# Gathering the rows of experts 4 to 7 in two halves of two experts, on one Trainium2 core

## The reference, cut to what matters

```python
expert = g_top * EXPERTS_PER_GROUP + top_i          # two experts for each token
xb = x_pad[idx]                                     # the rows of one expert
hb = jax.nn.silu(xb @ w_gate[e]) * (xb @ w_up[e])   # 1024 -> 512, twice
return hb @ w_down[e]                               # 512 -> 1024
y = jnp.zeros((n + 1, d), x.dtype).at[tok_pad].add(contrib)
```

## Time and profile before

| what | value |
|---|---|
| median of 3 runs | 1997.57 us (1997.38 to 1999.03) |
| the profiled execution's own time | 2002.36 us |
| its span in the profile | 2000.6 us |
| TensorE busy | 1926.9 us (96%) |
| VectorE busy | 803.8 us (40%) |
| ScalarE busy | 432.4 us (22%) |
| weight loads of experts (2 MB each) | 192 |

### The profile page before, as it was taken

The page is one execution under the profiler, slowest core; times in us unless marked ns, Lnnn a source line. Parts: engine busy times, 40 slices in busy tenths (PEclk is TensorE's granted clock), DMA queues, the critical chain, the costliest instruction groups (busy, mean ns, idle before and its releaser), DMA issues.

```text
span 2000.6 us, 21987 instructions
## 1 busy us (share of the span) xinstructions
PE 1926.9 (96%) x8606; PEld 1004.3 (50%) x8606; DVE 803.8 (40%) x2057; ACT 432.4 (22%) x883; POOL 87.5 (4%) x116
## 2 busy tenths in 40 slices
PE   8999999999999889999999999999988999999998
PEld 6886644444444335544454444444433564654555
DVE  4553454221111144455544422211114548874564
ACT  2000101111111024165310111111112532124454
POOL 0000000000000010023000000000001000000000
PEclk9999899999999899999999999999989999999999
DMA  7815489999999981121548999999999221120000
GB/s 309 195 69 231 167 338 405 428 427 427 428 428 427 425 345 67 73 85 42 230 169 346 408 428 427 428 428 429 427 424 358 79 90 67 60 85 1 12 11 22
DMA packets 48550, 512.32 MB, mean 256 GB/s; under 512 B 5296, under 2 KB 7472, under 8 KB 19248
## 3 DMA queue, kind: packets, MB, share of 16 engines
q1 hardware_dynamic: 39984, 480.86, 59.0%
q0 software_dynamic: 8448, 29.89, 3.9%
HBM read 484.38 MB, written 26.35 MB: 255 GB/s over the span
## 4 chain that ended last, share of the span: by engine, by line
PE 86%; DMA 5%; DVE 4%; ACT 2%; issue 2%; POOL 1%; SPq 0%; DVEq 0%; POOLq 0%; ACTq 0%
PE ps L1099 22%; PE ps L1138 10%; PE ps L1072 8%; PE ps L522 6%; PE ps L1949 6%; PE ps L728 5%; PE ps L1499 5%; PE ps L1666 3%; PE ps L2284 3%; PE ps L2147 3%; PE ps L1697 2%; DMA ring<-in_wexp 2%; PE ps L1163 1%; PE ps L2321 1%; PE ps L2302 1%
## 5 line engine op out<-in xcount | busy, mean ns | idle before, releaser
L1099 PE MATMUL ps<-ring,arena 128*48 128x512 f32 x1504 | 390.6, 607 | 29.4 <-issue 17.5
L1099 PEld LDWEIGHTS ps<-ring,arena 128*48 128x48 f32 x1504 | 116.3, 125 | 224.5 <-issue 223.1
L1112 DVE TENSOR_TENSOR arena<-arena,ps 48x512 f32<-48x512 f32 x64 | 44.2, 690 | 451.4 <-ACT arena L1106 451.3
L1072 PEld LDWEIGHTS ps<-arena,h 128*128 128x128 f32 x1024 | 158.6, 190 | 44.6 <-issue 44.6
L1138 PE MATMUL ps<-ring,arena 128*48 128x512 f32 x768 | 173.6, 592 | 1.1 <-ACT arena L1126 0.6
L1072 PE MATMUL ps<-arena,h 128*128 128x192 f32 (+1 forms) x1024 | 174.3, 325 | 0.0
L1099 PE MATMUL ps<-arena 128*48 128x512 f32 x544 | 173.0, 608 | 0.9 <-issue 0.9
L1106 ACT ACTIVATE arena<-ps 48x512 f32<-48x512 f32 x64 | 37.8, 590 | 465.4 <-PE ps L1099 465.4
L1949 PE MATMUL ps<-ring,arena 128*128 128x512 f32 (+3 forms) x384 | 132.7, 500 | 0.8 <-DVE arena L360 0.8
L1499 PE MATMUL ps<-ring,arena 128*128 128x512 f32 x256 | 114.0, 601 | 6.5 <-issue 3.3
L728 PE MATMUL ps<-ring,arena 128*128 128x512 f32 x256 | 112.8, 594 | 0.1
(11 more groups left out here) (301 smaller groups left out, 2307.7 us busy)
## 6 DMA issues: line engine op xcount, KB each, us to landing
ring<-in_wexp SPq DMA_DIRECT2D x142, 2048.0 KB, 19.5
arena<-in_wexp SPq DMA_DIRECT2D x50, 2048.0 KB, 16.1
ring<-in_wall SPq DMA_DIRECT2D x25, 2048.0 KB, 8.7
y_d<-arena POOLq DMA_DIRECT2D x60, 192.0 KB, 7.1
yo_d<-gbuf SPq DMA_DIRECT2D x2, 4032.0 KB, 46.4
ring<-in_wall SPq DMA_DIRECT2D x3, 1536.0 KB, 7.4
xs_d<-h POOLq DMA_DIRECT2D x8, 512.0 KB, 7.3
ring<-in_wall SPq DMA_DIRECT2D x4, 1024.0 KB, 7.4
```

The source lines that it names most:

```text
L1072: mm = pe.matmul(banks[4 + t % 2][:, k * 4 * CAP + z0:(k + 1) * 4 * CAP], h[:, i, kk * P:(kk + 1) * P], RT["sel"][:, NT * (p_ % 2) + i, z0 ...
L1099: mm = pe.matmul(outs[m], xeT[:, e_ // 4 % 2, k, e_ % 4 * CAP:(e_ % 4 + 1) * CAP], ws[m][:, k, :], start=(k == 0), stop=(k == KT - 1))
L1112: dve.tensor_tensor(hh[0:CAP, e_ % 2, :], sl[0:CAP, e_ % 2, :], banks[1][64:64 + CAP, :], ALU.mult).then_inc(S["hh"], 1)
```

## The change

The steps of a gather now carry the range of experts of the quad that they take, (p_, q_, za, zb). Quad 1 is gathered in eight steps of two experts (96 columns) instead of four steps of four (192 columns). The four steps of experts 4 and 5 stand at e = 2 and e = 3, where the whole quad's stood. The four of experts 6 and 7 stand at e = 4 (two) and e = 5 (two), ahead of quad 2's first and second step. `rows_done` gives the count of copies that an expert waits for, and quad 3's selection matrix is made at e = 6 instead of e = 4, since its buffer is read by quad 1 until e = 5.

```diff
+        XT_AT = [[], [(0, q_, 2, 4) for q_ in range(4)], [(1, 0, 0, 2), (1, 1, 0, 2)], [(1, 2, 0, 2), (1, 3, 0, 2)]]
+        XT_AT += [[(e_ // 4 + 1, e_ % 4, 0, 4)] if e_ // 4 + 1 < NE // 4 else [] for e_ in range(4, NE)]
+        XT_AT[4][0:0] = [(1, 0, 2, 4), (1, 1, 2, 4)]
+        XT_AT[5][0:0] = [(1, 2, 2, 4), (1, 3, 2, 4)]
+        XT_NO = {step: t for t, step in enumerate(step for steps_ in XT_AT for step in steps_)}
+
+        def rows_done(e_):
+
+            if e_ < 2:
+                return 2
+            return 3 + max(t for (p_, q_, z0, z1), t in XT_NO.items() if p_ == e_ // 4 and z0 <= e_ % 4 < z1)
+
+
+        SEL_AT = {1: 2, 6: 3}
+        SEL_AT.update({4 * p_ - 8: p_ for p_ in range(4, NE // 4)})
...
-        def pe_xt(pe, l, p_, q_):
-            t = 4 * p_ + q_
-            z0 = 2 * CAP if p_ == 0 else 0
+        def pe_xt(pe, l, p_, q_, za, zb):
+            t = XT_NO[p_, q_, za, zb]
+            z0, z1 = za * CAP, zb * CAP
...
-                    mm = pe.matmul(banks[4 + t % 2][:, k * 4 * CAP + z0:(k + 1) * 4 * CAP], h[:, i, kk * P:(kk + 1) * P], RT["sel"][:, NT * (p_ % 2) + i, z0:],
+                    mm = pe.matmul(banks[4 + t % 2][:, k * 4 * CAP + z0:k * 4 * CAP + z1], h[:, i, kk * P:(kk + 1) * P], RT["sel"][:, NT * (p_ % 2) + i, z0:z1],
...
-            pe.wait_ge(*M("xtc", l, 1 if e_ < 2 else 4 * (e_ // 4) + 6))
+            pe.wait_ge(*M("xtc", l, 1 if e_ < 2 else rows_done(e_)))
...
-                if e_ == 1 or e_ >= 4 and e_ % 4 == 0 and e_ // 4 + 2 < NE // 4:
-                    dve_sel(dve, l, e_ // 4 + 2)
+                if e_ in SEL_AT:
+                    dve_sel(dve, l, SEL_AT[e_])
```

More of the change, by code:

```diff
@@ L113, in build @@
         yo_d = [dram(f"yo_d{l}", [CAP * NOVF, D]) for l in range(2)]
-        LAYER = dict(gu=NE, sl=NE, hh=NE, ht=NE, hTc=NE, dn=NE, ya=NE, yb=NE, xt=NE + 2, xtc=NE + 2, sel=NE // 4 + NT, pp=8, ppc=8, cmb=8, pg=8, pl_t=8, sg=8,
+        LAYER = dict(gu=NE, sl=NE, hh=NE, ht=NE, hTc=NE, dn=NE, ya=NE, yb=NE, xt=NE + 6, xtc=NE + 6, sel=NE // 4 + NT, pp=8, ppc=8, cmb=8, pg=8, pl_t=8, sg=8,
                      ple_h=8, r_mm=4, r_lg=4, r_oh=4, r_cum=3, r_cnt=5, r_dif=2, r_exp=2, hot=8, ixmm=1, ix=1, ovf=1, tw=1, tt=1, ttc=1, tmm=8, tadd=8,
@@ L1040, in build @@
         PT_AT = 11
-        XT_AT = [[], [(0, 0), (0, 1), (0, 2), (0, 3)], [(1, 0), (1, 1)], [(1, 2), (1, 3)]]
-        XT_AT += [[(e_ // 4 + 1, e_ % 4)] if e_ // 4 + 1 < NE // 4 else [] for e_ in range(4, NE)]
+        XT_AT = [[], [(0, q_, 2, 4) for q_ in range(4)], [(1, 0, 0, 2), (1, 1, 0, 2)], [(1, 2, 0, 2), (1, 3, 0, 2)]]
[9 more added lines that the diff above has]
+        SEL_AT.update({4 * p_ - 8: p_ for p_ in range(4, NE // 4)})
         def hT_of(j):
@@ L1055, in dve_sel @@
             if p_ >= 2:
-                dve.wait_ge(*M("xt", l, 4 * (p_ - 2) + 6))
+                dve.wait_ge(*M("xt", l, rows_done(4 * (p_ - 2) + 3)))
             for i in range(NT):
@@ L1071, in pe_xt, with dve_xt @@
                 for i in range(NT):
-                    mm = pe.matmul(banks[4 + t % 2][:, k * 4 * CAP + z0:(k + 1) * 4 * CAP], h[:, i, kk * P:(kk + 1) * P], RT["sel"][:, NT * (p_ % 2) + i, z0:],
+                    mm = pe.matmul(banks[4 + t % 2][:, k * 4 * CAP + z0:k * 4 * CAP + z1], h[:, i, kk * P:(kk + 1) * P], RT["sel"][:, NT * (p_ % 2) + i, z0:z1],
                                    start=(i == 0), stop=(i == NT - 1))
             mm.then_inc(S["xt"], 1)
-        def dve_xt(dve, l, p_, q_):
-            t = 4 * p_ + q_
-            z0 = 2 * CAP if p_ == 0 else 0
+        def dve_xt(dve, l, p_, q_, za, zb):
+            t = XT_NO[p_, q_, za, zb]
+            z0, z1 = za * CAP, zb * CAP
             g = gain_cols(1 + 3 * l)[:, 2 * q_:2 * q_ + 2]
@@ L1082, in dve_xt @@
                 dve.wait_ge(*M("gu", l, 4 * (p_ - 2) + 4))
-            dve.tensor_tensor(xeT[:, p_ % 2, 2 * q_:2 * q_ + 2, z0:], banks[4 + t % 2][:, 0:8 * CAP].rearrange("p (k c) -> p k c", k=2)[:, :, z0:],
-                              g.unsqueeze(2).broadcast_to([P, 2, 4 * CAP - z0]), ALU.mult).then_inc(S["xtc"], 1)
+            dve.tensor_tensor(xeT[:, p_ % 2, 2 * q_:2 * q_ + 2, z0:z1], banks[4 + t % 2][:, 0:8 * CAP].rearrange("p (k c) -> p k c", k=2)[:, :, z0:z1],
+                              g.unsqueeze(2).broadcast_to([P, 2, z1 - z0]), ALU.mult).then_inc(S["xtc"], 1)
         def pe_gu(pe, l, e_):
@@ L1173, in dve_turn @@
             st = steps(dve)
-            dve.wait_ge(*M("xt", l, NE + 2))
+            dve.wait_ge(*M("xt", l, NE + 6))
             st.did(dve.memset(selw, 0.0))
@@ L1220, in pe_moe @@
                     pe_down(pe, l, e_ - 1)
-                for p_, q in XT_AT[e_]:
-                    pe_xt(pe, l, p_, q)
+                for step in XT_AT[e_]:
+                    pe_xt(pe, l, *step)
                 if e_ == 7:
@@ L1264, in dve_moe @@
                     dve_down(dve, l, e_ - 1)
-                for p_, q in XT_AT[e_]:
-                    dve_xt(dve, l, p_, q)
-                if e_ == 1 or e_ >= 4 and e_ % 4 == 0 and e_ // 4 + 2 < NE // 4:
-                    dve_sel(dve, l, e_ // 4 + 2)
+                for step in XT_AT[e_]:
+                    dve_xt(dve, l, *step)
+                if e_ in SEL_AT:
+                    dve_sel(dve, l, SEL_AT[e_])
                 next(places, None)
@@ L1338, in ovf_begin @@
                 e.wait_ge(*M("xs", l, 16 * NT))
-                e.wait_ge(*M("xtc", l, NE + 2))
+                e.wait_ge(*M("xtc", l, NE + 6))
                 e.wait_ge(*M("hTc", l, OVF_AT + 1))
```

## The result

The changed kernel is slower by a little: 2002.66 us median of 20 runs (1997.82 to 2010.6) against 1997.21 us for the kernel before (20 runs, 1994.34 to 2000.77), ratio 1.0028, 95% interval 1.0020 to 1.0037. A second set of runs on another occasion, 11 of them, gave 1.0014 (1.0005 to 1.0023). So the two sets put the cost of the change at 0.14% and 0.28%, 2.8 and 5.6 us, and their intervals reach from 1.0 to 7.4 us; forecast were 2.9.

A forecast was written before the change was run, and what follows sets the result against it. The weight stream was taken to bound each layer, with time changing only at its pauses. Shifts of +1.3 us in layer 0 and +1.6 in layer 1 gave 1997.57 + 2.9 = 2000.5 us, range 1997.8 to 2003.8.

The forecast's parts named there:

- a smaller margin: At expert 9, less margin than taken: 1 us a layer more, +4.9 us in all; chance 0.12.
- What bounds the layer: Each layer ends when its weight stream ends; time is won or lost only where the stream pauses.
- The rest of TensorE's lag: Late in a layer, lag above the stream's shift (3.6 - 1.3) goes in TensorE's own waits for weights, about 2.3 us.
- TensorE's terms: Two 96-column steps take 3.66 us; TensorE stands -3.7 us from expert 4, 0.0 from expert 5, +3.6 from expert 6.
- The old pauses: Stream pauses at 300 and 315 us, worth 1.0 and 1.5 us, both go as TensorE is earlier.
- The first and second new pause: At experts 5 and 6, TensorE's shift less the margin puts the stream at -1.6, then +0.5 us.
- The third new pause: At expert 9, near 390 us in layer 0: stream shift of +1.3 us there and +1.6 us in layer 1.
- the 15.4 us: Landing time of a weight load on an empty queue, from loads of 15.3 and 15.5 us; anything above is margin.
- the margin at expert 9: How much later its load may be issued without a pause: 2.3 us in layer 0, 2.0 in layer 1.
- Rival A: Layer end hangs on TensorE, so its lag passes whole: 3.64 us a layer, 2004.9 us; chance 0.12.
- Rival C: No third pause at expert 9; the two before it cancel what was won: +0.5 a layer, 1998.6 us; chance 0.2.
- rival B: In the gather steps, a half-width matmul costs half (169 ns): -2.5 us a layer, 1992.6 us; chance 0.06.

The follow-up runs named there:

- e3: The changed kernel with all eight steps of quad 1's gather at e = 2 and e = 3, four at each; ratio 1.0035 to the kernel before.
- e6: The changed kernel with quad 3's gathers put later, to e = 10 and 11, and 128 instructions more in each layer's jumped-over block; ratio 1.0000 to the kernel before.
- e1: The changed kernel with 128 TensorE instructions more in each layer's first overflow block, which is jumped over; ratio 1.0013 to the kernel before.
- e7: The changed kernel unaltered, run again on another occasion; ratio 1.0014 to the kernel before.

## Why the prediction was right, and which term was too small

It held in its mechanism and in its direction, and was low by the last term: forecast were +2.9 us, the two layers measured +4.2, and the two sets of runs 2.8 and 5.6. What came is nearest to the case that the forecast gave 0.12, a smaller margin and +4.9 us.

- **What bounds the layer**: right. In e3 and e6 only gather steps were moved, and the layer follows the pauses of the stream. The rest of TensorE's lag went in its own waits, as said, but less of it and earlier: before experts 25 and 26 of layer 0 it waited 0.58 and 1.46 us, in the changed kernel 0 and 0.85, so 1.2 us were taken up where 2.3 were forecast. The 4.85 us before expert 29 lie behind that.
- **TensorE's terms**: right to 0.1 us for a pair of half steps (3.74 for 3.66). The lag from expert 6 on was measured as 352.44 - 274.99 = 77.45 us from expert 2 to expert 7, against 73.74 before (350.87 - 277.13), +3.7 for +3.64.
- **The old pauses**: gone, both. The one of expert 2 stayed, as it had to.
- **The first and second new pause**: right in place and, within what the measure can tell, in sum. With them alone a layer stands at +0.5 and +0.7 (e6), forecast +0.5.
- **The third new pause, "Expert 9: +1.3 in layer 0 and +1.6 in layer 1"**: the term that was mis-sized. Measured +2.4 and +1.7, once more +2.5 and +1.9, and +3.1 and +2.0 in e1, which runs the same instructions. What failed in layer 0 is the 15.4 us that I took for a landing on an empty queue. In the changed kernel the loads behind the three new pauses of layer 0 land as follows:

```profile
L235 SPq DMA_DIRECT2D arena<-in_wexp x1: 328/328/328, 332.2 to 332.2; - x1
DMA to landing us min/median/max: 15.7/15.7/15.7
L235 SPq DMA_DIRECT2D ring<-in_wexp x1: 328/328/328, 349.4 to 349.4; - x1
DMA to landing us min/median/max: 14.4/14.4/14.4
...
L235 SPq DMA_DIRECT2D ring<-in_wexp x1: 327/327/327, 391.1 to 391.1; - x1
DMA to landing us min/median/max: 16.5/16.5/16.5
```

14.4 to 16.5 us, and the last of them took 16.6 us in e7 and 17.3 in e1, so a margin made with 15.4 is off by up to 1.9 us. With 16.5 the margin at expert 9 is 17.7 - 16.5 = 1.2 us and the shift 3.7 - 1.2 = +2.5, for a measured +2.4; with e1's 17.3 it is +3.3 for +3.1; in layer 1, where the load took 15.6 us, it is 3.7 - (17.4 - 15.6) = +1.9 against +1.7 and +1.9. These sums say which term was off and are no second proof: how much later a load lands is how much later it was issued plus how much longer it took. In layer 1 of the changed kernel's profile the whole shift is there before the third pause: the last load of expert 6's batch lands 91.1 us behind expert 2 (1148.3 + 16.8 - 1073.97) for 89.1 before (1146.6 + 18.5 - 1075.96), where the forecast has +0.5. In e7 it is +0.5 there and +1.8 behind expert 9. So in that one profile the match with +1.6 is luck. Why one such load takes 16.5 us I haven't tried. The two rows that I had of before (15.3 and 15.5) agreed by chance, and I took their spread for the uncertainty.
- **Rival A** is wrong in its mechanism: TensorE's lag of 3.7 us did not pass whole. Rival C is ruled out by the pause near 388 us and by the layers (e6 is what C would look like), rival B by e3 and by the 3.74 us.
- **Not foreseen**: the stop in expert 29. It is real, and of the cost above 2.9 us at most a part: by the layers alone, +4.2 us in both together, 0.21%, lies inside what the two sets of runs gave. I can't say from the runs whether it adds 0 or 1 us, or up to 1.6 by the later product of e1.

## What to carry to other kernels

Where a stream of transfers is full and an engine beside it frees its buffers, work taken off the engine early is worth only the pauses that it closes, and what is paid back later costs what it opens: list for each batch how late it may be issued, and set the engine's lag against that list up to the place where the lag is gone. Work that was put later can be put later still, to where the margins have grown; here two gather steps moved from experts 8 and 9 to 10 and 11 took the loss back, as far as layers and runs can tell. A margin worked out from two landings is good to 1 or 2 us, not to 0.1.

## What the runs showed of the hardware that I had not expected

Instructions that never run can stop an engine. With 128 instructions more in a block that TensorE jumps over, it stopped for 2.66 us behind the fifth matmul record of expert 29; with 160 it didn't, and with 0 it didn't. The trace has an instruction transfer of 16 KB under way in the stop. The page counts the instruction queues' transfers on the same 16 DMA engines as the weights, which are full at that time, and that is how I explain the length of the stop; it is argued and not shown, since no run had an idle stream there.
